# Moving the small block DMAs of a triangular inverse from SyncE's queue to GpSimd's queue

## The reference

```python
decay = jnp.where(tri, jnp.exp(jnp.where(tri, diff, 0.0)), 0.0)
k_beta = k * beta[..., None]
m = jnp.einsum('bhncd,bhnsd->bhncs', k_beta, k) * decay
m = jnp.where(tri_strict, m, 0.0) + jnp.eye(CHUNK, dtype=jnp.float32)
rhs = jnp.concatenate([v * beta[..., None], k_beta * jnp.exp(g)[..., None]], axis=-1)
sol = lax.linalg.triangular_solve(m, rhs, left_side=True, lower=True, unit_diagonal=True)
```

## Time and profile before

| | |
|---|---|
| median of 3 runs | 2593.26 us (2592.95 to 2595.0) |
| the profiled execution | 2584.58 us, its span 2582.8 us |
| mean granted clock of TensorE | 0.963 |
| PE busy | 2337.6 us, 91% |
| DVE busy | 1394.7 us, 54% |
| ACT busy | 927.3 us, 36% |
| POOL busy | 136.8 us, 5% |

### The profile page before, as it was taken

The page is one execution under the profiler, slowest core; times in us unless marked ns, Lnnn a source line. Parts: engine busy times, 40 slices in busy tenths (PEclk is TensorE's granted clock), DMA queues, the critical chain, the costliest instruction groups (busy, mean ns, idle before and its releaser), DMA issues. The chain is left out here.

```text
span 2582.8 us, 40809 instructions
## 1 busy us (share of the span) xinstructions
PE 2337.6 (91%) x14870; PEld 1931.1 (75%) x14870; DVE 1394.7 (54%) x2377; ACT 927.3 (36%) x1727; POOL 136.8 (5%) x187
## 2 busy tenths in 40 slices
PE   6799898998989898998999878999999999999687
PEld 3278786877768686877778757788887878878686
DVE  1343655555454555555564354656566665766554
ACT  3433324242423324242422253433424244242423
POOL 0000000000001000000100020000000000000002
PEclk8899999999999999999999989999999999999898
DMA  8964434352434445252545415533434344343453
GB/s 321 353 188 130 111 107 126 89 134 78 123 100 124 110 110 131 73 149 73 168 121 160 147 57 156 127 102 96 128 83 120 91 108 113 96 122 92 129 154 105
DMA packets 553603, 329.72 MB, mean 128 GB/s; under 512 B 48658, under 2 KB 517814, under 8 KB 552710
## 3 DMA queue, kind: packets, MB, share of 16 engines
q1 hardware_dynamic: 393174, 218.59, 30.5%
q10 hardware_dynamic: 160240, 109.13, 14.4%
q0 software_dynamic: 64, 0.20, 0.0%
HBM read 304.73 MB, written 23.13 MB: 127 GB/s over the span
## 5 line engine op out<-in xcount | busy, mean ns | idle before, releaser
L1699 PE MATMUL ps<-h_hi,w_hi 128*128 128x512 f32 (+1 forms) x2080 | 825.9, 397 | 17.6 <-DVE w_lo L1060 7.6
L1700 PE MATMUL ps<-h_lo,w_hi 128*128 128x512 f32 (+1 forms) x2080 | 765.1, 368 | 0.0
L1701 PE MATMUL ps<-h_hi,w_lo 128*128 128x512 f32 (+1 forms) x2080 | 764.2, 367 | 0.0
L1060 DVE TENSOR_TENSOR w_lo<-w_raw,w_hi 128x1024 fp32r<-128x1024 f32 (+1 forms) x332 | 399.2, 1202 | 345.9 <-ACT w_hi L607 280.0
L607 ACT CAST w_hi<-w_raw 128x1024 fp32r<-128x1024 f32 (+1 forms) x332 | 341.8, 1030 | 441.0 <-PE ps L1701 142.4
L1699 PEld LDWEIGHTS ps<-h_hi,w_hi 128*128 128x128 f32 x2080 | 398.4, 192 | 110.0 <-issue 42.6
L1701 PEld LDWEIGHTS ps<-h_hi,w_lo 128*128 128x128 f32 x2080 | 396.3, 191 | 67.5
L1700 PEld LDWEIGHTS ps<-h_lo,w_hi 128*128 128x128 f32 x2080 | 398.8, 192 | 46.5
L1060 DVE TENSOR_TENSOR arena<-arena,ps 128x512 f32<-128x512 f32 (+1 forms) x192 | 117.6, 640 | 107.4 <-PE ps L1790 106.0
L1959 PE MATMUL ps<-h_hi,w_hi 128*128 128x512 f32 (+1 forms) x448 | 160.6, 359 | 15.5 <-ACT arena L773 10.6
L1780 PE MATMUL ps<-arena 128*128 128x128 f32 x768 | 110.4, 290 | 55.6 <-DVE arena L1312 55.6
(11 more groups left out here) (191 smaller groups left out, 2740.4 us busy)
## 6 DMA issues: line engine op xcount, KB each, us to landing
w_raw<-in_w_in SPq DMA_DIRECT2D x260, 512.0 KB, 4.1
ada_raw<-in_w_ada ACTq DMA_DIRECT2D x128, 512.0 KB, 5.1
w_raw<-in_w_out SPq DMA_DIRECT2D x64, 448.0 KB, 3.7
arena<-in_w_ada SPq DMA_DIRECT2D x27, 512.0 KB, 8.3
w_raw<-in_w_ada SPq DMA_DIRECT2D x19, 512.0 KB, 8.5
ada_raw<-in_w_ada SPq DMA_DIRECT2D x18, 512.0 KB, 8.3
arena<-decay_rows ACTq DMA_DIRECT2D x16, 512.0 KB, 5.7
x_channel_major<-arena ACTq DMA_DIRECT2D x1, 4096.0 KB, 17.5
```

The lines of the kernel that those rows point to most:

```text
L1060: return V.tensor_tensor(o, a, b, op)
L1699: mm(o, w_hi[:, s, k], h_hi[:, kt, t0:], start=kt == 0, stop=False)
L1700: before_last = mm(o, w_hi[:, s, k], h_lo[:, kt, t0:], start=False, stop=False)
L1701: last = mm(o, w_lo[:, s, k], h_hi[:, kt, t0:], start=False, stop=kt == KT - 1)
```

## The change

The two DMA sequences move, unchanged in content, from SP's program to POOL's, behind the clearing of `solved` and `blk_s` and ahead of the powers of the two head norms. The tables that placed them in SP's program go away. POOL now waits in order for `m_ready`, `blocks_out`, `blocks_solved`, `solved_out` and `inv_cleared`. Buffers, semaphores, and the work of PE, DVE and ACT stay.

```diff
-        BLOCKS_OUT, BLOCKS_BACK = {0: 7, 1: 7}, {0: 10, 1: 10}
...
-        OUT_BLOCKS = {0: (7, 11), 1: (8, 13)}
...
-                def blocks_to_partitions(i):
-
-                    sp.wait_ge(m_ready, nth(layer, i, -1))
...
-                def blocks_back(i):
-
-                    sp.wait_ge(blocks_solved, nth(layer, i, -1))
...
-                        if fill and k == BLOCKS_OUT[layer]:
-                            blocks_to_partitions(i)
-                        if fill and k == BLOCKS_BACK[layer]:
-                            blocks_back(i)
...
                     G.memset(blk_s[:, 0::BLK + 1], 1.0).then_inc(blk_identity, 1)
                     pool.wait_ge(blk_identity, h())
 
+                    pool.wait_ge(m_ready, h())
+                    own.note()
+                    for b in range(NB):
+                        rows = slice(b * BLK, (b + 1) * BLK)
+                        pool.dma_start(blocks_of(m_dram, b),
+                                       m_upper.rearrange("p x c d -> p (x c) d")[rows, :, rows]).then_inc(blocks_out, 16)
+                    pool.wait_ge(blocks_out, h(-1, 16 * NB, 16 * NB))
+                    own.note()
+                    pool.dma_start(blk_m, m_dram).then_inc(blocks_in, 16)
+
+                    pool.wait_ge(blocks_solved, h())
+                    own.note()
+                    pool.dma_start(s_dram, blk_s).then_inc(solved_out, 16)
+                    pool.wait_ge(solved_out, h(-1, 16, 16))
+                    pool.wait_ge(inv_cleared, h())
+                    own.note()
+                    for b in range(NB):
+                        rows = slice(b * BLK, (b + 1) * BLK)
+                        pool.dma_start(solved.rearrange("p x c d -> p (x c) d")[rows, :, rows],
+                                       blocks_of(s_dram, b)).then_inc(inv_started, 16)
+
                     pool.wait_ge(oa_summed, h())
```

More of the change, by code:

```diff
@@ L574, in output_part @@
                                              y_dram[layer, ks, :, c0 * P:].rearrange("k p t -> p k t")).then_inc(y_loaded[g], 16)
[L575 to L578, removed]
                 def body(i, project, fill):
```

## The result

The changed kernel takes 2624.53 us (median of 4 runs, 2623.36 to 2626.18); the kernel before, run beside it, takes 2593.11 us. The ratio is **1.0126 [1.011, 1.0142]**: slower by 31 us. The forecast was 2659 us, slower by 66, with 2573 to 2728 as the range of 8 in 10. The side was right and the size twice too large. The cause was only in part the one forecast: the prediction put the loss down to slow issues on POOL, and it came mostly from SP's weight loads, which the prediction costed at nothing.

What follows compares the result with a forecast made beforehand. PE was taken as the bound. Layer 1's longer trip 64 us, layer 0's heads 1, the last heads 0 and 1: 66 us on 2593.26, so 2659 us, with 2573 to 2728 as the 8 in 10 range.

Steps and rivals of the forecast that it cites:

- Layer 1 has nothing to win and no slack: Layer 1: PE reaches L1780 when the transpose is just ready, so a longer trip costs PE 9.1 us a head.
- the term c: Block DMAs on POOL: time from one issue to the next, taken as 1.0 us against SP's 0.46.
- the low end: Lowest value considered for POOL's issue time, 0.73 us, from its only DMA in the trace, the mask load.
- the second rival: Both layers: low c with some e comes out near no change, 2586 us or some 2602; chance 0.12.
- the term e: Block trip: extra landing time after issue on POOL's queue over SP's, 0.6 us, four times in a trip.
- its first rival: The free queue wins, mainly through PE's wait in layer 0: faster, 2560 to 2582 us; chance 0.17.
- I cost that at nothing: SP's queue in the heads: earlier weight loads gain 0 us, as PE hardly waits for weights.
- span 8 us: Sign: the eight block stores on POOL take 8 us; 5.8 would be the free-queue case, 11.7 issue growing with pieces.
- From solution to first return it is 2.8 us in both layers: Sign on POOL: more than 4 us would mean that a queue of its own doesn't free the store.
- stays near 7 us a head in layer 0: Sign: PE's idle time before L1780, unchanged in layer 0 and appearing in layer 1, there 9 us perhaps shared with L1865.
- The third: POOL's issue time grows with a block DMA's pieces, c 1.46 and e 0.9: 194 us slower, 2787 us; chance 0.23.
- The fourth: SP's earlier loads help PE's waits for splits, at most 8 us off any case; no chance of its own.

Runs made afterwards that it cites:

- the s half: Against the kernel before, only the store of the solution and the eight returns moved to POOL, m's blocks still by SP: 2589.1 us, ratio 0.9991.
- both runs with extra issues: Kernel before with eight, or four, more small scratch DMAs on SP ahead of the returns in layer 1: 2643.65 us, or 2617.64 us.
- with SP held: Changed kernel, SP waiting before weight unit 7 until m's blocks are loaded and before unit 10 until the solved blocks have landed: 2589.78 us, ratio 0.9995.
- the m half: Against the kernel before, only the eight stores of m's blocks and the load into partitions moved to POOL: 2630.99 us, ratio 1.0152.
- returns at unit 9: Kernel before, all on SP, with layer 0's solved blocks going back ahead of weight unit 9 instead of unit 10: 2551.61 us, ratio 0.9851.

## Why the prediction came out as it did

**Right: who bounds and where the loss falls.** "Layer 1 has nothing to win and no slack" held, and the sum of 1:1 there as well. The mean trip in layer 1, from m to the transpose, is 34.2 us against 27.5 (seven heads, 6.7 more), and the mean head is 7.0 longer. Delays of the returns alone cost 1.1 to 1.2 times their length (the s half, and both runs with extra issues). Granted clocks behind such a stall in layer 1, before, then after:

```profile
1887.90:1891.00 3.10, 3.09 (x27) 3.09 (x28) 2.28 (x4) 1.63 (x3) 1.18 (x2) 1.00 0.48 140
```

```profile
1898.90:1902.00 3.10, 3.05 (x16) 3.06 (x17) 2.60 (x4) 0.13 (x1) 1.18 (x2) 0.60 0.00 0
```

Where PE came without a stall it ran 27 matmuls in 3.1 us at a clock of 1.00, and after 3.63 us of idling 16 at 0.60, mostly the lower of the two levels.

**Wrong: the term c.** "**c = 1.0**", with 0.73 as "the low end", measured 0.53. By the prediction's own price (224 us for each us of c in 14 heads) the 0.47 too much is 105 us. The low end was taken from POOL's single row, the masks, which in after still take 0.78. The fine pieces, the argument for going above, cost nothing. The Trainium skill (DMA: Bandwidth & Descriptors, Anatomy of one DMA), weighed in the second rival, says that many descriptors can be emitted before their cost shows; the trace agrees, since 128 pieces and 64 KB are issued in the same 0.54 to 0.56 us.

**Wrong: the term e**, in kind and not only in size. "What a transfer of POOL's queue takes longer to land" was a constant, 0.6 us, four times. It is two things. One is a reaction: POOL starts a DMA 0.65 us after the semaphore that releases it, as from the solution at 1887.54 + 0.19 = 1887.73 to its store at 1888.38, where SP takes 0.08. The other is the company. From the last store to the load's issue it is 1.8 us with SP held and 3.2 to 4.4 without (layer 1), 3.4 to 4.0 and 5.3 to 6.1 (layer 0); behind the last return 1.4 and 2.6 to 3.0 (layer 1). The one head of layer 1 in which POOL makes a gap of its own (last section) is left out of these. The Trainium skill (DMA: Bandwidth & Descriptors, Latency and other measured facts), as the prediction read it, would have had a constant 0.4 for e, from its first-byte figures. The run with SP held shows no such constant in layer 1: there the last landing is 1.37 us on POOL and 1.32 on SP. That four reactions of nearly 0.6 over SP's come to the same 2.3 us as four times e is luck.

**The failing steps** are two, and they pull opposite ways. The size failed at c: with 0.53 in place of 1.0 the prediction's own sum gives 66 - 105, some 39 us faster than before, which is its first rival. The side then hangs on the other step: "its weight loads no longer stand behind the waits ... I cost that at nothing; if that cover were thinner, the earlier loads could only help." With SP held the loss is gone. 2624.5 - 2589.8 = some 34 us hang on the released queue (the kernel before, run beside each, differs by 2 us), which is what the change costs as a whole; POOL's fixed costs in layer 1 and the free store in layer 0 about cancel. PE indeed didn't need the weights sooner (it waits 8.1 us for their splits in after, 7.6 before); but the loads delay the block transfers, in the stretch in which PE comes to wait for these. Whether they meet in the DMA engines, at a port or in DRAM no run tells. That "slower" came out right is luck: the two errors had opposite signs.

**How the errors met.** In layer 1 the m half was put at 3.4 us later and measured 3.3 (3.6 without the first head): the eight issues and the reaction 3.1 us shorter than assumed, the landings as much longer. The s half was put at 12.7 us from solution to transpose, and measured 10.4. That is 2.3 us a head, 16 us for 7 heads, and it is about the gap between the 65 forecast for layer 1 and the 49 measured. In layer 0 the s half measured 11.9 on average, 0.8 less than the sum's 12.7, and the heads won 7.4 us where the sum had a loss of 1. Start and end give -2.8. 66 - 16 - 8.4 - 2.8 = 38.8, the difference of the two spans. The released queue doesn't close the whole distance from the sum at c = 0.53: that would be some 51 us won in layer 0 and 11 lost in layer 1, and with SP held it is 17.9 and 26.8. In layer 0 the landings stay long in that run too.

**What would show it**, point by point. The eight stores "span 8 us": 4.25. The load "some 9.8 us after m": 8.4 in the head of layer 1 shown (m is written at 1864.65), 10.7 in that of layer 0 (844.29). "From solution to first return it is 2.8 us in both layers": 3.3 in layer 1, and 3.2 to 5.1 in layer 0, over 4 in three of seven heads; yet with that store on POOL it is still far from the 10.1 of before. PE's idle time before the inverse "stays near 7 us a head in layer 0": 3.8 to 6.1. It "appears in layer 1": 3.3 to 3.7 in six heads and 2.0 in the first. Of the 49 us that seven heads of layer 1 got longer PE is idle 31: 21 at the inverse, 4 at the mix (L1855, 35.0 against 31.2), which the prediction foresaw, 9.4 new at L1638, less what fell elsewhere. The other 18 are its matmuls (739.8 us busy, against 722.2), slower behind the stalls; for that the prediction has no term. POOL's norm powers behind the new waits cost nothing that shows in PE's waits.

**The rivals.** The first (the free queue wins) is real in layer 0 and outweighed in layer 1. Its decision point, c = 0.71 at e = 0.6, was passed by the measured c = 0.53, and the kernel was slower all the same: a threshold in c alone was no use once e depended on SP. The second (low c with some e, near no change) is passed by the measured c as well; its mechanism gives no loss. The third (issue grows with pieces) is out. The fourth ("SP's loads matter after all") had its sign wrong: they do matter, against the change.

## What to carry to other kernels

- When a queue is freed, write down what it will start in the time that it gains, and which transfers on the critical path that meets. Here 512 KB loads landing beside 8 KB blocks cost as much as the change lost, and two plain waits on the freed queue gave it back.
- Before a transfer is given another queue, look at its place in its own. One number in the order table, 10 to 9 in one layer, took away 38 of PE's 53 us of waiting and made this kernel 1.5% faster.
- Take an issue cost from an instruction of the same shape, or leave the range open on both sides.

## What the runs showed of the hardware

- POOL issues a block DMA (8 KB in 128 pieces) in 0.53 us and a 64 KB one in 0.54 to 0.56 (0.62 where only the s half is on POOL); SP takes 0.46 and 0.48. A copy of 8 KB from one DRAM tensor to another took SP 0.64 us to issue.
- POOL starts 0.65 us after a semaphore releases it, SP 0.08 us.
- The queue part of the profile's page of after has these blocks in few packets: without the masks' 64 packets and 0.20 MB 9,216 for 4.21 MB, some 457 bytes each, where the queue of SP lost 39,424 (393,174 less 353,750) for 4.21 MB, some 107 bytes each. No run shows that time hangs on it.

```profile
q1 hardware_dynamic: 353750, 214.38, 29.0%
...
q0 software_dynamic: 9280, 4.41, 1.0%
```

- A block DMA that lands in 1.7 to 1.9 us alone takes 3.5 to 3.6 beside one or two 512 KB loads, whether POOL sends it beside SP's load (after) or SP beside ACT's loads (returns at unit 9).
- POOL makes a gap of 2.7 us behind its 120th DMA of the program, counted with the masks, and one of 2.5 behind its 236th. It is so in the three kernels with all 288 block DMAs on POOL; the two with one half on POOL (145 DMAs) have the first gap alone, and the one with 73 has none. Nothing in the profile releases it; it goes by the count, and its cause stays open. POOL's timeline of a late head of layer 0 in after:

```profile
1163.75 0.56 POOL L1578 DMA_DIRECT2D arena<-s_blocks  x1 [3.91 <-DMA s_blocks<-arena]
1167.03 3.66 POOL L1578 DMA_DIRECT2D arena<-s_blocks  x7 [2.71 <-issue]
```
